# State-space tiles issued in pairs on a quarter of the TensorE array, and a reordered second normalisation, in a hybrid attention, state-space and expert kernel

## The reference

```
hn = rmsnorm(h) * g_mix ; proj = hn @ w_in          # q, k, v, f, u, gate
att: 8 heads x 64, logits + cumulated log forget gate, causal, softmax, times v
ssm: 32 groups x 16 channels, one 64-dim complex diagonal state per group:
     x_t = a * x_(t-1) + B u_t ;  y_t = Re(C x_t) + D u_t ;  z = gelu(y)
     branch = (z @ w_glu_val) * sigmoid(z @ w_glu_gate)
h = h + (g0 * (att @ w_att) + g1 * branch) @ w_out
hn = rmsnorm(h) * g_ffn ; q = hn @ w_query           # 8 heads x 2 halves x 128
     scores against 128 keys per half, top 16 of each, top 16 of the sums -> 128 experts per frame
h = h + sum_k softmax_k * gelu(u_k . hn) * v_k       # u, v: 16384 x 1024 each
out = rmsnorm(h) * g_out
```

## Time and profile before

| | |
|---|---|
| median of three runs | 1726.26 us |
| profiled execution, its span | 1727.33 us, 1725.0 us |
| TensorE busy | 1622.8 us (94%) |
| VectorE busy | 1184.2 us (69%) |
| GpSimd busy | 883.3 us (51%) |
| ScalarE busy | 342.8 us (20%) |
| moved by DMA | 489.47 MB |
| indirect gathers of expert rows | 512 |

### The profile page before, as it was taken

One profiled execution on the slowest core, in us unless ns is written; L12 is line 12 of the kernel. 1 busy time (PEld: TensorE's weight loads), 2 busy tenths in 40 slices (PEclk: granted clock), 3 DMA queues, 4 the chain that ended last, 5 costly groups with the idle time before them and its releaser, 6 DMA issues.

```text
span 1725.0 us, 20488 instructions
## 1 busy us (share of the span) xinstructions
PE 1622.8 (94%) x6590; PEld 1159.5 (67%) x6590; DVE 1184.2 (69%) x2625; ACT 342.8 (20%) x783; POOL 883.3 (51%) x1117
## 2 busy tenths in 40 slices
PE   7989999999899989987799999999999999999997
PEld 5768887686687658876366666666666666666664
DVE  4656488569664559799766766766666666667666
ACT  3244331212343112388000000001000000000001
POOL 6756566348653337600745544545654455445442
PEclk9999999999999989999899999999999999999999
DMA  6422235344897964200999999999999999999997
GB/s 211 122 74 74 68 122 153 113 156 135 295 323 273 352 219 135 85 0 9 399 409 409 409 409 409 409 409 409 408 409 403 408 409 408 409 409 407 409 408 270
DMA packets 139100, 489.47 MB, mean 284 GB/s; under 512 B 16497, under 2 KB 17009, under 8 KB 138881
## 3 DMA queue, kind: packets, MB, share of 16 engines
q0 software_dynamic: 73728, 268.47, 39.7%
q1 hardware_dynamic: 65280, 219.85, 35.0%
HBM read 483.53 MB, written 4.72 MB: 283 GB/s over the span
## 4 chain that ended last, share of the span: by engine, by line
DMA 40%; PE 33%; DVE 12%; POOL 7%; issue 5%; ACT 2%; SPq 1%; DVEq 0%; POOLq 0%; ACTq 0%
DMA ring<-in_expert_v,chosen 23%; DMA ring<-in_expert_rows,chosen 16%; PE pair L723 15%; PE pair L735 4%; POOL ring L692 4%; DVE ring L1476 4%; DVE ring L1473 3%; PE pair L1029 2%; PE pair L770 1%; DVE temp L1712 1%; PE pair L756 1%; PE pair L1013 1%; PE pair L816 1%; PE pair L793 1%; PE pair L971 1%
## 5 line engine op out<-in xcount | busy, mean ns | idle before, releaser
L692 POOL DMA_INDIRECT ring<-in_expert_rows,chosen x256 | 286.5, 1119 | 359.8 <-DVE ring L1473 320.2
L1013 PE MATMUL pair<-temp,hnT 128*128 128x512 f32 x984 | 445.5, 595 | 25.8 <-DVE hnT L1352 21.8
L1476 DVE SCALAR_TENSOR_TENSOR ring<-ring,chosen 128x1024 f32<-128x1024 f32 x256 | 328.9, 1285 | 156.6 <-DMA ring<-in_expert_v,chosen 154.0
L1004 PE MATMUL pair<-hnT,temp 128*128 128x256 f32 x1904 | 430.4, 379 | 0.0
L1004 PEld LDWEIGHTS pair<-hnT,temp 128*128 128x128 f32 x1904 | 361.8, 190 | 100.0 <-issue 56.9
L1473 DVE SCALAR_TENSOR_TENSOR ring<-ring 128x1024 f32<-128x1024 f32 x256 | 311.1, 1224 | 131.2 <-DMA ring<-in_expert_rows,chosen 130.0
L692 POOL DMA_INDIRECT ring<-in_expert_v,chosen x256 | 266.7, 1042 | 251.2 <-DVE ring L1476 230.1
L1013 PEld LDWEIGHTS pair<-temp,hnT 128*128 128x128 f32 x984 | 182.9, 190 | 224.5 <-issue 213.8
L1326 ACT ACTIVATE hnT<-pair 128x256 f32<-128x256 f32 x119 | 45.7, 384 | 811.7 <-PE pair L1004 685.1
L723 PE MATMUL pair<-hnT,gate_all 128*128 128x256 f32 x592 | 135.3, 385 | 1.4 <-issue 1.4
L723 PEld LDWEIGHTS pair<-hnT,gate_all 128*128 128x128 f32 x592 | 112.6, 194 | 16.5 <-issue 1.7
(11 more groups left out here) (292 smaller groups left out, 1925.0 us busy)
## 6 DMA issues: line engine op xcount, KB each, us to landing
temp<-in_expert_v SPq DMA_DIRECT2D x128, 512.0 KB
temp<-in_expert_u SPq DMA_DIRECT2D x119, 512.0 KB
gate_all<-in_w_query SPq DMA_DIRECT2D x27, 512.0 KB
ring<-in_w_g SPq DMA_DIRECT2D x16, 512.0 KB, 3.5
gate_all<-in_w_g SPq DMA_DIRECT2D x11, 512.0 KB
gate_all<-in_expert_u SPq DMA_DIRECT2D x9, 512.0 KB
ring<-in_w_u SPq DMA_DIRECT2D x8, 512.0 KB, 4.1
ring<-in_w_k SPq DMA_DIRECT2D x8, 512.0 KB, 4.0
```

Source lines behind the costliest of these rows:

```text
L692: pool.indirect_dma_start(out=gathered[:, g % SLOTS, :], out_offset=None, in_=(expert_rows, expert_v_rows)[part], in_offset=bass.IndirectO ...
L1004: mm = pe.matmul(u_out[n % 2], u_in[:, n % 2, c * P:(c + 1) * P], hnT[:, c, FIRST[1]:L], start=(c == 0), stop=(c == DC - 1))
L1013: mm = pe.matmul(pairs[i][:, b * 512:(b + 1) * 512], weighed[n][:, i * P:(i + 1) * P], v_in[:, n % 2, b * 512:(b + 1) * 512], start=False, ...
L1476: dve.scalar_tensor_tensor(out=fin, in0=slot, scalar=wsel[:, at:at + 1], in1=fin, op0=ALU.mult, op1=ALU.add).then_inc(row_done, 1)
```

## The change

The zero-padded `b_chunk` goes. `b_times_u` takes one or two tiles and uses B's 32 rows as they lie, against the 32 channels of the tile; `c_times_x` takes two tiles and writes each tile's 32 outputs to its own 32 partitions of one bank. Pairs of tiles are issued together (single b products are left for tiles 12 to 15 of the second half). `xs` is doubled, and `evac_y` copies two tiles at once. PSUM places follow: in the first half the attention products share pair 0, by single banks, and pairs 1 and 2 hold B u of two tiles.

In the second half's norm, the features of tile 2 are written right behind its norm, its transposes stand between the halves of tile 3's output product, and the first two queries are done for tile 2 before tile 3 is normalised. `ROWS_BEFORE_QUERY` is 21: 7 rows ahead of each residual sum, 7 behind the last features.

```diff
-ROWS_PER_STEP, ROWS_PER_MERGE, ROWS_BEFORE_QUERY = 3, 1, 16
+ROWS_PER_STEP, ROWS_PER_MERGE, ROWS_BEFORE_QUERY = 3, 1, 21
+TILE_QUERIES = 2
...
-        xs = [temp[:, 6 * W0 + a * HALF:6 * W0 + (a + 1) * HALF] for a in range(2)]
+        xs = [[temp[:, at + a * HALF:at + (a + 1) * HALF] for a in range(2)] for at in (6 * W0, T_LOOP + SLOT)]
...
-                if n >= 1:
-                    filled(pool, ("y", (n - 1) // NT, (n - 1) % NT))
-                chain(pool.tensor_tensor(xs[0], pa, pb, ALU.subtract))
+                if n >= 2:
+                    filled(pool, ("y", hf, i - 2 - i % 2) if i >= 2 else ("y", 0, NT - 2))
+                chain(pool.tensor_tensor(xs[i % 2][0], pa, pb, ALU.subtract))
...
-            def b_times_u(hf, i):
-                drained(pe, ("u", hf, i // 4))
-                pe.wait_ge(b_chunk_ready, hf * NT + i + 1)
+            def b_times_u(hf, *tiles):
+                for i in tiles:
+                    drained(pe, ("u", hf, i // 4))
                 for a, kind in enumerate(("bu_re", "bu_im")):
-                    name = (kind, hf, i)
-                    vacant(pe, name)
-                    pe.matmul(pair(name)[:, 0:WIDTH[hf]], b_chunk[:, i % 4, a, :], uT[hf][:, i // 4, :],
-                              start=True, stop=True).then_inc(full_sem(name), 1)
+                    for i in tiles:
+                        vacant(pe, (kind, hf, i))
+                    for i in tiles:
+                        name, q = (kind, hf, i), slice(32 * (i % 4), 32 * (i % 4) + 32)
+                        pe.matmul(pair(name)[:, 0:WIDTH[hf]], bT[q, a, i // 4, :], uT[hf][q, i // 4, :],
+                                  start=True, stop=True).then_inc(full_sem(name), 1)
...
-                four = [cd[:, a, c:c + 4, :].rearrange("p a b -> p (a b)") for a in range(2)]
-                pe.matmul(y, four[0], xs[0], start=True, stop=False)
-                pe.matmul(y, four[1], xs[1], start=False, stop=True).then_inc(full_sem(name), 1)
+                for a in range(2):
+                    for i in tiles:
+                        q = slice(32 * (i % 4), 32 * (i % 4) + 32)
+                        mm = pe.matmul(pair(name)[q, 0:HALF], cd[:, a, i, :], xs[i % 2][a], start=(a == 0), stop=(a == 1))
+                mm.then_inc(full_sem(name), 1)
...
-                        if hf == 0:
-                            c_times_x(0, i - 1)
+                        if hf == 0 and i % 2 == 0:
+                            c_times_x(0, i - 2, i - 1)
                         gate_part(hf, i - 1, 3)
-                    if hf == 0 and i + 1 < NT:
-                        b_times_u(0, i + 1)
+                    if hf == 0 and i % 2 and i + 1 < NT:
+                        b_times_u(0, i + 1, i + 2)
...
-                    c_times_x(1, c + 1)
-                    b_times_u(1, c + 3)
+                    if c % 2:
+                        b_times_u(1, c + 3, c + 4)
+                    else:
+                        c_times_x(1, c, c + 1)
...
-                if c + 9 < NT:
-                    c_times_x(1, c + 9)
-                if c + 11 < NT:
-                    b_times_u(1, c + 11)
+                if c % 2 == 0:
+                    c_times_x(1, c + DC, c + DC + 1)
+                if c + 12 < NT:
+                    b_times_u(1, c + 12)
...
+            a, z = TILES[1]
+            output_half(a, 0)
+            output_half(a, 1)
+            output_half(z, 0)
+            second_norm(a)
+            output_half(z, 1)
+            drained(pe, ("hn2", a))
+            for n in range(TILE_QUERIES):
+                query_of_tile(n, a)
+            second_norm(z)
             queries(1)
...
-                        if hf == 0 and i + 4 < NT:
-                            next_b_chunk(i + 4)
...
-                        rows_to(EARLY - ROWS_BEFORE_QUERY + 8 * (i % 2 + 1))
+                        rows_to(EARLY - ROWS_BEFORE_QUERY + 7 * (i % 2 + 1))
...
+                    if hf:
+                        to_features(("hn2", i), hnT[:, :, FIRST[1] + (i % 2) * P:FIRST[1] + (i % 2 + 1) * P], P, gffn)
```

More of the change, by code:

```diff
@@ L135, in hybrid_program @@
         inputs_of = lambda h, i: [(("bu_re", h, i), (2, 0)), (("bu_im", h, i), (2, 1))]
-        output_of = lambda h, i: [(("y", h, i), (3, 1))]
+        inputs_of_two = lambda h, i: [((kind, h, i + k), ((2, 3 if h else 1)[k], a))
+                                      for a, kind in enumerate(("bu_re", "bu_im")) for k in range(2)]
+        output_of = lambda h, i: [(("y", h, i), (1, 1) if h and i < DC else (3, 1))]
+        turn = lambda n: (0, n % 2) if hf == 0 else "turn"
         if hf == 0:
-            order += inputs_of(0, 0)
+            order += inputs_of_two(0, 0)
@@ L145, in hybrid_program @@
+                order += output_of(0, i - 2) if hf == 0 and i % 2 == 0 else []
                 order += [(("gate", hf, i - 1), (3, 0))]
-            if hf == 0 and i + 1 < NT:
-                order += inputs_of(0, i + 1)
+            if hf == 0 and i % 2 and i + 1 < NT:
+                order += inputs_of_two(0, i + 1)
         a, b = TILES[hf]
         if hf == 0:
-            order += [(("u", 1, 0), "turn")]
-            for k in range(3):
-                order += [(("u", 1, k + 1), "turn")] + inputs_of(1, k)
@@ L847, in branches_first @@
             def branches_first():
-                inputs("u", 1, 0)
-                for k in range(3):
-                    inputs("u", 1, k + 1)
-                    b_times_u(1, k)
-                c_times_x(1, 0)
+                for k in range(SC):
+                    inputs("u", 1, k)
+                    if k % 2:
+                        b_times_u(1, k - 1, k)
                 for j, h in heads[0][-HEADS:]:
@@ L875, in second_norm, with query_of_tile @@
                 transposes(("hn2", i), hn_tile[i % 2], P)
+            def query_of_tile(n, i):
+                name, lo = ("qry", 1, n), i % 2 * P
+                slot, landed, v = weight_at[name]
+                if i == TILES[1][0]:
+                    vacant(pe, name)
+                    pe.wait_ge(landed, v)
+                w = slot.rearrange("p (k m) -> p k m", m=P)
+                for c in range(DC):
+                    mm = pe.matmul(pair(name)[:, lo:lo + P], w[:, c, :], hnT[:, c, FIRST[1] + lo:FIRST[1] + lo + P],
+                                   start=(c == 0), stop=(c == DC - 1))
+                if i == TILES[1][1]:
+                    mm.then_inc(full_sem(name), 1)
             def queries(hf):
@@ L1163, in mixer @@
                     evac_u(1, 0)
-                    for n in range(NT, NT + 4):
-                        next_b_chunk(n)
                     gelu_z(0)
@@ L1514, in add_skip @@
             def add_skip(hf, c):
-                for i in range(4 * c, 4 * c + 4):
+                for i in (4 * c, 4 * c + 2):
                     drained(dve, ("y", hf, i))
```

109 lines of the change are left out of this document (44 added, 65 removed).

## The result

The changed kernel takes 1709.5 us (median of four runs, 1708.2 to 1712.5) against 1726.4: a ratio of 0.990 (0.987 to 0.993), 16.9 us less. In three more series it came to 0.991, 0.990 and 0.990 of the kernel before, each with an interval of about 0.0015 either way. The forecast was 1701.5 with a range of 1690 to 1719: the sign and the range held, a third of the gain is missing. Each stage runs from the first start of a named piece of work to that of the next, read from the timelines of the two executions.

What follows compares the result with a forecast made beforehand. TensorE bounds the first mixer loop, VectorE the list searches, DMA the last stage. Gains 9.2 + 2.2 + 2.9 + 4 + 6.5 = 24.8 us give 1702.5 profiled, 1701.5 median; own range 1697 to 1706, whole range 1690 to 1719.

Steps and rivals of the forecast that it cites:

- eight slots become five: First mixer loop: paired products overlap only partly, being two instructions each, saving 3/8 per pair, 10.0 us in all.
- shape changes, 15 groups: First mixer loop: each group changes the array's shape twice at 0.08 us, costing 2.4 us (0 to 4.8).
- ScalarE's copies, for which L814 waited: First mixer loop: copies of B's weights go, so TensorE's wait at L814 goes, gaining 1.6 us.
- Nothing else is late next: First mixer loop: no other engine holds TensorE up, VectorE being busy 62 and GpSimd 64 of 104 us.
- Only these 2.2 us can go: First-half branches: VectorE runs back to back, so only its waits for TensorE, 0.6 and 1.6 us, can be gained.
- first list 637.4 instead of 639.13: Second norm and queries: VectorE's first list search starts at 637.4 us, with two scores waiting; part of a 4 us gain.
- Last stage: Final stage, full of DMA transfers: moving 5 of 443 late rows ahead saves 1.29 us each, 6.5 us.
- whole overlap: Rival on paired products: they save half; first loop gains 15.0, output projection 5, total 32.7 us, 1694; chance 0.25.
- stages 2 and 3: First-half branches and first output projection, forecast to gain 2.2 and 2.9 us.
- No overlap: Rival on paired products: nothing runs side by side; total gain 9.7 us, 1717 (1715 to 1720); chance 0.28.
- shape changes above 0.26 us each: Rival, loop and output projection: without overlap, 46 changes above this make the kernel slower; at 0.5 us, 1737; chance 0.04.
- the third rival: Second norm: rows wait for transfers and lists start late; stage loses 3 instead of gaining 4, 1708; chance 0.08.

Runs made afterwards that it cites:

- The shorter states: Changed kernel with GpSimd's turning back of the state cut from six operations to two for second-half tiles 0 to 10 (states wrong); 1701.5 us, single run.
- the forms: Changed kernel with first-loop groups issued on one quarter, one behind the other, four at once, singly or twice; B pair on one quarter 2.03 us, four at once 0.67.
- the reordered kernels: Three variants of the changed kernel: loop C pair behind the fourth gate part, output blocks waiting per merged chunk, output-projection C pairs moved; 1713.1, 1715.3 and 1715.1 us.
- chain_first: Changed kernel with loop C pair behind fourth gate part, waits per merged chunk, B of tile 11 behind block 0, other C pairs moved; 1715.1 us (1709.9 beside it).

## Why the prediction was right or wrong

**First mixer loop, 9.2 forecast, 8.6 measured.** The mechanism, overlap of products on different quarters, is right, and so is the statement that the number of instructions stays. The sizes of the terms are wrong, and that the sum came out so near is luck. The count "eight slots become five" is wrong: it is four. A group pays 0.4 us (B) or 0.34 (C) for its shape where 0.16 was forecast, some 0.18 a change, above the bound of 0.16. From the loop's first full step on (105.97 before and 104.91 after, each to `u`) 103.26 us became 95.54, 7.7 less. By the forecast's terms, from start to start:

| term | forecast | measured |
|---|---|---|
| overlap of pairs | 10.0 | 12.6 |
| shape changes, 15 groups | -2.4 | -5.5 |
| ScalarE's copies, for which L814 waited | 1.6 | 3.5 |
| new waits | 0 | -3.0 |

The new waits are 1.8 us for GpSimd's state and 1.2 us for the bank of the gate (three gaps of 0.3, and 0.05 in each odd step), against "Nothing else is late next". The 3.5 us stand in the gaps from start to start ahead of L814; the brackets of the earlier trace rows show 1.6 of them. The terms add up to 7.6 of the 7.7; the other 0.9 us of the stage lie ahead of the first full step and were not taken apart.

**Branches, 2.2 forecast, 0.4 measured.** The failed step is "Only these 2.2 us can go", read as if they would go whole. The waits went (the 1.6 for projections and the 0.6 for B of the earlier trace rows are no longer there), but VectorE now waits 0.6 for GpSimd and its merge products meet GpSimd more often: L1359 on two SBUF operands grew from 0.72 to 0.94 us, eight times, 1.7 us; L1510 adds 0.5. Merge products that read PSUM got 0.7 shorter. The shorter states show that GpSimd is the cause of these lengths.

**First output projection, 2.9 forecast, -0.4 measured.** C in pairs saves 7 x 0.865 - 4 x 0.99 = 2.1 and the fifth B tile 0.87. Against them stand the single B tiles, which I priced as wide ones (0.86; 1.05 to 1.18, so 0.9 more for four), the products ahead of and behind eight groups (1.0), and a first block mostly at half clock (5.4 instead of 3.5 us, 1.9), because TensorE now comes 2.35 us early for the last merge instead of 0.4. Waits are about as before in sum (1.14 and 0.89 instead of 2.1), the 0.9 for the last state as forecast; the 1.14 for the bank I had not seen.

**Second norm and queries, 4 forecast, 4.2 measured.** Second sum and first score came within 1 us of their places. The step "first list 637.4 instead of 639.13" failed: the features were written 0.6 us later than forecast, the last row waited 1.28 us for its transfer, and the list started 0.2 us later than before, counted from the output product. The gain stands ahead of the first score (41.65 instead of 46.32 us behind the output product); from there to the chunks ahead it takes 57.25 us instead of 56.77. VectorE's 13.7 us of waits for scores went, as I said, and its last step ends 2.5 us earlier.

**Last stage, 6.5 forecast, 4.9 measured.** Rate and share are as before (405 GB/s, 1.02), so the mechanism held. The executions give 5.4 us for five rows, but with their spread it stays open whether a row is worth 1.08 or the forecast's 1.29 us.

Of the rivals, whole overlap was right about the array and wrong about the time: it left the price of a shape and the new waits out of the loop, and stages 2 and 3 did not let its gain through. No overlap is excluded by the forms, and shape changes above 0.26 us each by the 0.17 to 0.2 that one costs. A row did come late and so did the first list, yet the stage gained 4.2, so the third rival fell.

## What to carry to other kernels

A pair of products on different quarters costs as much as one, and four as much as two, but a group costs 0.3 to 0.4 us beside its slots, so it wants as many tiles as banks allow; a single tile on a quarter is slower than the wide form. Before counting a gain on one engine, list what lies a microsecond behind it in that stage: here a bank still being copied, a merge on VectorE and a state on GpSimd each took back part of what TensorE saved. A wait of TensorE is paid twice where products at half clock follow it, so a reordering that makes one can be dearer than the wait it removes.

## What was not expected of the hardware

Products queued one tile behind the other, four instructions on one quarter and then four on the next, ran side by side (1.13 us for eight slots of 0.227). The 2.35 us wait of TensorE ahead of the first output block was followed by half clock in all four executions of the changed kernel, while the 0.4 us wait there before was not; waits of 2.10 and 4.67 us in the reordered kernels were, one of 2.31 us in `chain_first` was not. A wait of 1.23 us near 257 us was followed by a granted clock of 0.63 and 0.52 from 258 to 262 us in `chain_first`, one of 1.25 at the same place in the changed kernel by 1.00. So the length of a wait alone doesn't tell what follows; why was not tried. VectorE's operations on two SBUF operands take 0.42 us alone and up to 0.97 beside GpSimd.
